# Inputs loaded already transposed, gathered pairs' places freed by their last readers, and the first mixer ahead of the second block's attention on TensorE

## What is computed

```python
# first block, depth 1
h = rmsnorm(x, mix_norm_g)
proj = h @ w_in                       # q, k, v of three branches, and the gates
o = gates[0]*(moba @ w_a) + gates[1]*(dilated @ w_d) + gates[2]*(memory @ w_m)
mkv = rmsnorm(mem, mem_norm_g) @ w_mem_kv     # keys and values of the memory branch
x = x + o @ w_out
x = x + gated_ffn(rmsnorm(x))         # 22 up tiles, 3-tap conv, 11 down slabs
# second block, two layers
for l in range(2):
    x = x + concat(attention, conv, recurrence) @ w_out_2[l]
    h2 = rms_norm(x, norm2_g)
    q = h2 @ peer_wq[l]               # scores against 2 x 128 keys, top 16 twice
    # e: 128 experts per token, g: their softmax weights
    x = x + sum_k g[k] * gelu(h2 . u_tab[e[k]]) * v_tab[e[k]]
return rms_norm(x, final_g)
```

## Time and profile before

| | us |
|---|---|
| median of 3 runs | 2021.88 |
| lowest and highest run | 2019.99, 2023.11 |
| the profiled execution | 2020.95 |
| its span, first to last instruction | 2019.2 |

### The profile page before, as it was taken

The page is one execution under the profiler, slowest core; times in us unless marked ns, Lnnn a source line. Parts: engine busy times, 40 slices in busy tenths (PEclk is TensorE's granted clock), DMA queues, the critical chain, the costliest instruction groups (busy, mean ns, idle before and its releaser), DMA issues.

```text
span 2019.2 us, 21790 instructions
## 1 busy us (share of the span) xinstructions
PE 1767.6 (88%) x7152; PEld 1002.5 (50%) x7152; DVE 1282.8 (64%) x3502; ACT 870.7 (43%) x2188; POOL 593.2 (29%) x517
## 2 busy tenths in 40 slices
PE   9999999999899889888779988977898888777776
PEld 4459865763487446455226545622364464222222
DVE  4324337578665448786786866688677687865444
ACT  2423214344477433823344473344445634443333
POOL 0000000033222224343343424344433335443331
PEclk9999999999999999999899999999999989999999
DMA  9669877479999999999999999999999999999996
GB/s 389 212 261 357 300 278 253 153 283 419 419 419 419 420 420 419 419 417 417 420 420 412 419 419 408 419 420 420 420 420 420 364 420 417 421 419 420 420 420 266
DMA packets 108385, 770.14 MB, mean 381 GB/s; under 512 B 12144, under 2 KB 12656, under 8 KB 16368
## 3 DMA queue, kind: packets, MB, share of 16 engines
q0 software_dynamic: 73728, 536.90, 64.4%
q1 hardware_dynamic: 34544, 231.85, 29.7%
HBM read 767.65 MB, written 1.05 MB: 381 GB/s over the span
## 4 chain that ended last, share of the span: by engine, by line
DMA 50%; PE 34%; DVE 7%; ACT 4%; issue 3%; POOL 1%; SPq 0%; DVEq 0%; POOLq 0%; ACTq 0%
DMA arena<-in_peer_dram,eidx 15%; DMA ring<-in_peer_dram,eidx 14%; DMA kv<-in_peer_dram,eidx 12%; PE psum L1190 8%; PE psum L755 8%; PE psum L778 7%; DMA ring<-in_slabs_dram 5%; DMA early<-in_peer_dram,eidx 4%; PE psum L990 4%; PE psum L1007 2%; DVE arena L2109 1%; PE psum L961 1%; DVE ring L2109 1%; ACT diag L1535 1%; DVE kv L2109 1%
## 5 line engine op out<-in xcount | busy, mean ns | idle before, releaser
L2262 POOL DMA_INDIRECT arena<-in_peer_dram,eidx x205 | 240.8, 1175 | 796.0 <-DVE eidx L1981 411.4
L1190 PE MATMUL psum<-arena,diag 128*128 128x512 f32 x704 | 345.6, 617 | 72.4 <-ACT diag L1535 70.7
L1525 ACT ACTIVATE wexp<-wexp 128x1 f32<-128x1 f32 x512 | 103.1, 201 | 683.8 <-DVE wexp L2109 678.3
L2109 DVE CUSTOM_DVE_ANT_0 arena<-arena,osb 128x1024 f32<-128x1024 f32 x205 | 250.1, 1223 | 155.0 <-DMA arena<-in_peer_dram,eidx 153.8
L1190 PE MATMUL psum<-ring,diag 128*128 128x512 f32 x568 | 279.4, 618 | 53.1 <-ACT diag L1535 52.4
L2109 DVE CUSTOM_DVE_ANT_0 ring<-ring,osb 128x1024 f32<-128x1024 f32 x152 | 185.6, 1222 | 108.8 <-DMA ring<-in_peer_dram,eidx 108.5
L2262 POOL DMA_INDIRECT ring<-in_peer_dram,eidx x152 | 171.7, 1130 | 281.0 <-PE psum L1190 231.6
L1190 PEld LDWEIGHTS psum<-arena,diag 128*128 128x128 f32 x704 | 125.4, 192 | 254.5 <-ACT diag L1535 146.8
L755 PE MATMUL psum<-ring,hT 128*128 128x512 f32 x528 | 237.8, 597 | 13.6 <-DMA ring<-in_slabs_dram 12.2
L1190 PE MATMUL psum<-kv,diag 128*128 128x512 f32 x368 | 183.3, 624 | 40.4 <-ACT diag L1535 40.1
L1190 PEld LDWEIGHTS psum<-ring,diag 128*128 128x128 f32 x568 | 102.5, 194 | 200.5 <-ACT diag L1535 110.1
(11 more groups left out here) (340 smaller groups left out, 2025.1 us busy)
## 6 DMA issues: line engine op xcount, KB each, us to landing
ring<-in_slabs_dram SPq DMA_DIRECT2D x200, 1024.0 KB, 6.0
ring<-in_slabs_dram SPq DMA_DIRECT2D x8, 768.0 KB, 4.2
kept<-in_slabs_dram SPq DMA_DIRECT2D x4, 1024.0 KB, 13.4
arena<-in_peer_dram,eidx POOLq DMA_INDIRECT x205
ring<-in_peer_dram,eidx POOLq DMA_INDIRECT x152
ring<-in_slabs_dram SPq DMA_DIRECT2D x4, 512.0 KB
kk<-in_keys_dram SPq DMA_DIRECT2D x2, 1024.0 KB
kv<-in_peer_dram,eidx POOLq DMA_INDIRECT x104
```

Source lines behind the costliest of these rows:

```text
L1190: ins = pe.matmul(bank(b), diags_of(n), pair(slot_of[n])[:, 1024 + 512 * h:1536 + 512 * h], start=(k == 0), stop=(k == 127))
L1525: act.activation(wn, wn, ACT.Gelu_apprx_tanh).then_inc(*up("gelu", n))
L2109: v.tensor_tensor_reduce(out=row, in0=row, in1=row_y[t], scale=1.0, scalar=0.0, op0=ALU.mult, op1=ALU.add, accum_out=wexp[:, c:c + 1]).the ...
L2262: pool.indirect_dma_start(pair(i), None, tables, bass.IndirectOffsetOnAxis(ap=eidx[:, 128 * t + k:128 * t + k + 1], axis=0)).then_inc(sig. ...
```

## The change

Three things change, and the order of all engines is planned anew.

1. The host also hands over `xT` and `memT`, the inputs `x` and `mem` with features on the partitions. SP loads them into the places of the transposed tiles, and `scale_input` multiplies them by the gain on DVE in place. The 32 transposes, their banks and the 9 spare products on the identity go. The plain `x` and `mem` are still loaded, for the norms and the residual. The first slab is loaded in two halves with the second half of `xT` between them, and SP's first loads are put in another order. Of the second tile of `xT`, the load waits for the memory products, since it takes the place of `memT`.
2. Each place waits for the last instruction that reads what lies in it (`SLOT_FREE`). M00's tile `mixT` moves within `arena` to suit that.
3. `T_ATT` goes from 49 to 0: from the query products on, M00 never stands behind B1 on TensorE.

```diff
-T_... T_QUERY, T_ATT, ... = ... 64, 49, ...
+T_... T_QUERY, T_ATT, ... = ... 64, 0, ...
-        ARENA_FREE = (("wq", "M00", 0), ("wq", "M00", 3), ("key_scores", "M00", 3), ("key_scores", "M00", 3))
+        SLOT_FREE = (("o_turn", "M00"), ("wout", "M00", 1), ("wq", "M00", 3), ("key_scores", "M00", 3),
+                     ("att_scores", "B1", 7), ("att_values", "B1", 7), ("att_counted", "B1", 5, 1))
...
-                elif i < 4:
-                    w.wait_ge(*at(*ARENA_FREE[i]))
                 elif i < 7:
-                    w.wait_ge(*at("att_over", 1))
+                    w.wait_ge(*at(*SLOT_FREE[i]))
...
-            "M00": Room(..., arena[:, 0:2816], arena[:, 3072:5120], arena[:, 5120:8192]),
+            "M00": Room(..., arena[:, 0:2816], arena[:, 4096:5120], arena[:, 5120:8192], arena[:, 2816:3840]),
...
+            def scale_input(turned, gain, loaded, *key):
+                w.wait_ge(sig.sem("l_v"), 16)
+                w.wait_ge(*loaded)
+                g_ = gain.unsqueeze(2).to_broadcast(list(turned.shape))
+                v.tensor_tensor(turned, turned, g_, ALU.mult).then_inc(*up("scaled_in", *key))
...
-                    yield from turn_tile(s, x3[:, t, :], b_[6:8], "turned_v", (sig.sem("l_x0"), 16), "h")
-                    turns(b_[5], START[1])
-                    w.wait_ge(*at("turned_v", s, "h", 1))
+                    w.wait_ge(*at("scaled_in", "x0", 0))
...
+                    w.wait_ge(*at("mem_kv", 1))
+                    sp.dma_start(arena[:, 7168:8192], T["xT"][1]).then_inc(sig.sem("l_tx1"), 16)
```

More of the change, by code:

```diff
@@ L186, with __init__ @@
 class Room:
-    def __init__(self, order, S, T, O, scr, hT, tmp):
+    def __init__(self, order, S, T, O, scr, hT, tmp, mixT=None):
         self.bank, self.S, self.T, self.O = order, S, T, O
+        self.mixT = hT[:, 1024:2048] if mixT is None else mixT
         self.scr, self.hT, self.tmp = scr, hT, tmp
@@ L474, in make_plan @@
             used, loaded, taken, holding = {}, [], [0], {s: [] for s in STAGES}
-            slots, pairs = {0: ("free", 0), 1: ("free", 1), 2: ("free", 2), 3: ("free", 3), 4: ("att_over", 1), 5: ("att_over", 1), 6: ("att_over", 1)}, {}
+            slots, pairs = dict(enumerate(SLOT_FREE)), {}
             landed, counts, tensor = {}, {"dot": 0, "weigh": 0}, []
@@ L486, in signal @@
                 asleep.clear()
-                for i in range(4):
-                    if key == ARENA_FREE[i]:
-                        seen["free", i] = when + T_HOP
             def request(queue, n, when, mb):
@@ L754, in token_tile @@
                         w.wait_ge(*after)
+                    if n == 0 and k == 2 and not measured:
+                        w.wait_ge(sig.sem("slab%d" % place(0)), 16)
+                    if key == (0, 0) and name == "qkv" and k == 4:
+                        w.wait_ge(*at("scaled_in", "x0", 1))
                     ins = pe.matmul(bank(b), hT_[:, k, :], wk[:, k % 4, :], start=(k == 0), stop=(k == 7))
@@ L901, in block @@
                 if t == 0:
-                    for u in range(2):
-                        yield from turn_tile(s, mem3[:, u, :], b_[6:8], "turned_v", (sig.sem("l_m"), 16), "m%d" % u)
-                    w.wait_ge(*at("turned_v", s, "m1", 1))
+                    w.wait_ge(*at("scaled_in", "mem"))
                     for part in range(2):
@@ L1013, in block @@
                     bank_free[b_[6 + h]] = at("ffn_x", t, h)
[L1015 to L1024, removed]
-                    bank_free[b] = at("turned_v", "B1", "h", h)
             early_weights = {}
@@ L1456, in mixer @@
                 if l == 0:
-                    before.append(at("turned_v", "B0", "m1", 1))
+                    before.append(at("mem_sq", 1))
                 else:
@@ L1722, in block @@
                     begin(s)
-                    yield from turn_tile(s, "h", vecs[:, V_MIX:V_MIX + 8], b_[6:8], hTt)
+                    for h in range(2):
+                        scale_input(hTt[:, 4 * h:4 * h + 4, :], vecs[:, V_MIX + 4 * h:V_MIX + 4 * h + 4], (sig.sem(("l_tx0", "l_txr")[h]), 16), "x0", h)
+                        yield
                 yield from rms_tile(s, "h", "rms", s)
@@ L1805, in block @@
                 if t == 0:
-                    for u in range(2):
-                        yield from turn_tile(s, "m%d" % u, vecs[:, V_MEM:V_MEM + 8], b_[6:8], memT[:, :, 128 * u:128 * u + 128])
+                    scale_input(memT, vecs[:, V_MEM:V_MEM + 8], (sig.sem("l_tmem"), 16), "mem")
+                    yield
                 yield from norms(1)
@@ L2276, in slab @@
                     w.wait_ge(*at(*consumed.get(before(n), ("ffn_down", 1, 10))))
+                if n == 0:
+                    sp.dma_start(slot(0)[:, 0:1024], T["slabs"][i][:, 0:1024]).then_inc(sig.sem("l_first"), 16)
+                    sp.dma_start(hT[:, 512:1024], T["xT"][0][:, 512:1024]).then_inc(sig.sem("l_txr"), 16)
+                    sp.dma_start(slot(0)[:, 1024:width], T["slabs"][i][:, 1024:width]).then_inc(sig.sem("slab%d" % place(0)), 16)
+                    return
                 sp.dma_start(slot(n)[:, 0:width], T["slabs"][i][:, 0:width]).then_inc(sig.sem("slab%d" % place(n)), 16)
@@ L2519 @@
     arrays = {
-        "x": a["x"][0], "mem": a["mem"][0], "pos": a["positions"][0].reshape(2, P).T,
+        "x": a["x"][0], "xT": a["x"][0].reshape(2, P, 8, P).transpose(0, 3, 2, 1).reshape(2, P, 1024),
+        "mem": a["mem"][0], "memT": a["mem"][0].reshape(256, 8, P).transpose(2, 1, 0).reshape(P, 2048), "pos": a["positions"][0].reshape(2, P).T,
         "const": constants(), "vecs": vecs, "rows": np.broadcast_to(row, (P, row.size)),
```

56 lines of the change are left out of this document (31 added, 25 removed).

## The result

The changed kernel takes 2031.3 us (median of 4 runs, 2028.97 to 2033.71), the kernel before 2022.18 us in the same comparison: a ratio of 1.0048, with a 95% interval of 1.0035 to 1.0062. It is slower by half a per cent, where 2016 us had been forecast. The profiled execution took 2032.07 us, 11.1 us more than the one of before. The time went in the first quarter of the span.

The account below looks back on a forecast made before the run. TensorE was taken to bound the kernel up to T, DMA bytes and gaps after it. Attention +14, gathers -15, ramp -3 and late plan -1 gave -5 us from 2020.95, so 2016 us, range 2007 to 2025.

Parts of the forecast that it names:

- The start: From the first loads to the query products: memory products and `wq` start 2.2 us earlier, `wq` at 376.2 us.
- The routing: Beside the query products: first gather leaves at 402.7 us, 9.6 us earlier; the fourth at 410.
- Gathers by T: Gathers landed when B1's gate products start: 7 instead of 1, 15 us won.
- T: Start of B1's gate products, 425.97 us before: forecast at 440 us, 14 us later.
- the eight units: B1's attention, now alone behind `wq`: 3.2 us per unit, 25.6 us in all.
- the tail with the output: End of B1's attention: 5 us for the tail plus 1 us for transposing the output.
- The ramp: DMA engines filling up just behind B1's gate start: 3 us won, from 0 to 5, with two gathers in flight.
- The late plan: The rest, planned anew, with M11's first routing near 1600 us: 1 us won, between 5.8 won and as much lost.
- the second rival: Gain given back: a stall like that at M11's routing returns elsewhere, 2022 us, no difference; chance 0.20.
- The fall of the clock: Rival in B1's attention: TensorE's clock falls, gates start at 451, 2027 us, slower; chance 0.18 including other late gate starts.

Follow-up runs that it names:

- B: The changed kernel with places 0 to 6 freed as before, attention still alone behind the query products and inputs loaded transposed: 2029.41 us, ratio 1.0040.
- F: The changed kernel with 5 identity products ahead of each of the eight groups of transposes in B1's attention: 2028.19 us, ratio 1.0033.
- G: The changed kernel with the planner putting pairs ahead of everything from B1's gates on until 48 gathers are out: 2024.76 us, ratio 1.0024.
- C: The kernel before with only T_ATT set to 0, inputs and places as before: 2028.01 us, ratio 1.0045.
- I: The changed kernel with the two products of pairs in B1's attention moved behind B1's first gates: 2034.39 us, ratio 1.0068.

## Why the prediction was wrong

- **The start** was sized at 2.2 us, at the memory products and at `wq`. The traced execution shows nothing at the former (50.87 us in both) and 0.7 at `wq` (377.73 us against 378.42), but its memory products were the latest of all with this start. Over the twelve traces with the loaded transposes the median is 49.5 us for the memory products, 1.4 earlier, and 377.3 for `wq`, where the two with the old start have 378.3 and 378.4: about 1 us, half of the forecast. The forecast let the first loads move 274 to 416 GB/s; between 3 and 7 us they moved 201 to 282.
- **The routing** was right: the first gather was forecast at 402.7 us and left at 403.53; four were out at 411.69 (forecast 410). One sum was off: `wq`'s start and terms add up to 408.9 us, which was put down as about 408.
- **Gathers by T** were right: seven landed, 15 us forecast and 16.4 measured, with parts of the two in flight. The comparison behind them was too narrow, though: B shows that most of the seven come from the early end of `wq`, thus from the third part, and not from the new places.
- **T** was forecast at 440 (14 us later) and measured at 446.54 (20.6). In the terms of its sum, `wq` ended 1.3 us later (409.26 us, forecast at 408), the eight units took 29.5 us instead of 25.6, and the tail with the output took 7.9 instead of 6. Up to 3.8 us of the miss are the clock's (F); the rest has no experiment of its own.
- **The ramp** was the step that decided. I credited 3 us, which is the whole loss of before, because two gathers would be in flight at T, and so assumed full DMA engines from there on. The 9.4 us of loss behind T cost 7.0 more than before, a miss of 10 us. I had counted landed gathers as time won and not asked who empties their places; TensorE's rows behind T, in the order that was there to read, had no pair for 29 us. G shows it: with that order mended the loss behind T is 1.9 us, and the change gains 5 us by the ratios and 6.5 by the medians, with intervals that only just part. Where the places come free as before, in B and C, the loss is 2.1 and 1.8 us.
- **The late plan** was forecast at -1 and came to nothing: the hole of before around 1600 us is smaller, 2.7 us of loss between 1590 and 1640 instead of 6.4, and between 840 and 900 us 4.6 us are lost that were 0.2. A stall thus returned elsewhere, as the second rival has it (4.4 us of its 5.8).
- **The sum of the misses.** 6.6 us on T, 10 on the ramp and 1 on the late plan, less 1.4 on the gathers, make 16.2 us; 16.1 lie between the forecast of 2016 and the profiled 2032.07.
- **The rivals.** The fall of the clock came as described, with 0.50 where 0.58 had been seen, and the sign was that rival's. Its price was not: T at 446.5 and not 451, and of the time at most 2 to 3 us, which F's interval doesn't tell from nothing. The Trainium skill, "TensorE: Matmul & The Clock Gate", section "HAM oscillation — how this bites in real kernels", says that short bursts of matmuls between waits run at the half rate. The windows of I from 415 to 430 us agree, with 0.50 and TensorE busy for 3.4 to 3.9 of each 5 us; from 430 to 445 us the change runs at 0.50 with hardly a wait. The Trainium skill, "TensorE: Matmul & The Clock Gate", section "Part 4: PE-mode transpose", says that transposes don't count as busy in the same way; no run here separates them from the short products beside them.

## What to carry to other kernels

A transfer that comes earlier is won only if the place that it fills is emptied earlier too: read what follows on the consuming engine before counting landed bytes as time. Where the second half of a kernel is bound by bytes, compare the bytes moved by a fixed moment behind the change; here this gave the end within about 3 us for thirteen kernels with T anywhere from 424 to 451 us. And a chain of small steps over three engines was cheap here only while another stage's work filled its gaps: alone, it put T off by 18 to 21 us (B, C and the change).

## What was not expected of the hardware

- The granted clock stayed at 0.50 from 430 to 445 us with TensorE busy for 14.2 of 15 us; the longest idle time of TensorE before it fell was 2.5 us. Five identity products per unit held it at 1.00 (F). With the same order, it fell at other moments in another execution (G). With the pair's product between two units it was 0.70 to 0.96 from 415 to 430 us, and without it 0.50 (I); in B, with that product, it was 1.00 up to 425 us and 0.50 after.
- The first loads moved 203 GB/s between 3 and 7 us, and 201 to 282 over the twelve traces with this start, against 334 and 331 with the old one, though SP issued the first seven at about 0.5 us each. Whether that is the form of the transposed loads or their size was not tried.
